# A two-layer decoder step with streamed weights: the stream numbered across layers, fewer semaphore clears, reordered sums, and the rounding of the weights moved from POOL to ACT

## What is computed

```python
mod = (cs @ w_ada[l] + b_ada[l])[:, None, :]
sh_m, sc_m, gt_m, sh_f, sc_f, gt_f = jnp.split(mod, 6, axis=-1)
h = _rmsnorm(x, norm_mix[l]) * (1.0 + sc_m) + sh_m
mix, states = _token_mixers(h, ...)      # h @ w_in, three mixers, gates, @ w_out
x = x + gt_m * mix
h = _rmsnorm(x, norm_ffn[l]) * (1.0 + sc_f) + sh_f
x = x + gt_f * _swiglu(h, w_gate_up[l], w_down[l])
```

## Time and profile before

| | |
|---|---|
| median of three runs | 2710.65 us (2705.59, 2710.65, 2713.01) |
| profiled execution | 2709.27 us, its span 2707.5 |
| mean granted TensorE clock | 0.962 |
| moved by DMA | 263.94 MB, 97 GB/s on average |

### The profile page before, as it was taken

One profiled execution on the slowest core, in us unless ns is written; L12 is line 12 of the kernel. 1 busy time (PEld: TensorE's weight loads), 2 busy tenths in 40 slices (PEclk: granted clock), 3 DMA queues, 4 the chain that ended last, 5 costly groups with the idle time before them and its releaser, 6 DMA issues. The chain is left out here.

```text
span 2707.5 us, 48025 instructions
## 1 busy us (share of the span) xinstructions
PE 2527.8 (93%) x20318; PEld 2412.4 (89%) x20318; DVE 1032.3 (38%) x1481; ACT 456.8 (17%) x856; POOL 1546.9 (57%) x1292
## 2 busy tenths in 40 slices
PE   5989999999999899999969899999999997999997
PEld 3878898989989889999958799889899797999997
DVE  4654414250833442222256634331427435222223
ACT  2432222121021120000024222310211212000000
POOL 2542234557547757777745322356664585777774
PEclk8999998999999999999989899999999998999999
DMA  8730013222423512322256200142141241223222
GB/s 315 242 104 28 28 40 99 81 66 87 113 59 114 223 59 87 86 90 90 79 186 212 73 32 28 47 125 75 63 137 52 57 151 56 90 85 90 88 86 73
DMA packets 167045, 263.94 MB, mean 97 GB/s; under 512 B 14128, under 2 KB 83376, under 8 KB 165040
## 3 DMA queue, kind: packets, MB, share of 16 engines
q1 hardware_dynamic: 166832, 260.88, 30.4%
HBM read 239.65 MB, written 21.17 MB: 96 GB/s over the span
## 5 line engine op out<-in xcount | busy, mean ns | idle before, releaser
L730 PE MATMUL gemm_psum<-h_hi_lo,w_hi_lo 128*128 128x272 f32 x12000 | 1633.1, 295 | 60.2 <-POOL w_hi_lo L707 41.2
L730 PEld LDWEIGHTS gemm_psum<-h_hi_lo,w_hi_lo 128*128 128x128 f32 x12000 | 1561.7, 193 | 107.9 <-issue 52.9
L705 POOL TENSOR_TENSOR w_hi_lo<-w_raw,consts 128x512 fp32r<-128x512 f32 (+1 forms) x644 | 686.2, 1066 | 1080.6 <-PE gemm_psum L730 984.8
L707 POOL TENSOR_TENSOR w_hi_lo<-w_raw,w_hi_lo 128x512 fp32r<-128x512 f32 (+1 forms) x644 | 861.8, 1338 | 50.4
L1894 ACT ACTIVATE tiles<-gemm_psum 128x544 f32<-128x544 f32 (+1 forms) x188 | 116.5, 624 | 1189.6 <-PE gemm_psum L730 1189.0
L730 PE MATMUL gemm_psum<-ffn_hi_lo,w_hi_lo 128*128 128x272 f32 x2112 | 266.5, 288 | 0.0
L730 PEld LDWEIGHTS gemm_psum<-ffn_hi_lo,w_hi_lo 128*128 128x128 f32 x2112 | 266.1, 188 | 0.0
L1876 DVE TENSOR_TENSOR tiles<-gemm_psum,tiles 128x544 f32<-128x544 f32 x44 | 31.9, 725 | 392.9 <-PE gemm_psum L730 392.9
L730 PE MATMUL gemm_psum<-o_hi_lo,w_hi_lo 128*128 128x272 f32 x1152 | 154.0, 290 | 0.0
L730 PEld LDWEIGHTS gemm_psum<-o_hi_lo,w_hi_lo 128*128 128x128 f32 x1152 | 147.1, 189 | 0.0
L1894 ACT ACTIVATE scratch<-mix_psum 128x512 f32<-128x512 f32 (+3 forms) x112 | 58.8, 547 | 367.7 <-PE mix_psum L994 172.8
(11 more groups left out here) (236 smaller groups left out, 1935.9 us busy)
## 6 DMA issues: line engine op xcount, KB each, us to landing
w_raw<-in_w_gu SPq DMA_DIRECT2D x176, 256.0 KB, 2.7
tiles<-in_w_ada SPq DMA_DIRECT2D x64, 512.0 KB, 4.3
w_raw<-in_w_merge SPq DMA_DIRECT2D x96, 256.0 KB, 2.6
w_raw<-in_w_first SPq DMA_DIRECT2D x68, 256.0 KB, 5.1
w_raw<-in_w_ret SPq DMA_DIRECT2D x64, 256.0 KB, 2.7
w_raw<-in_w_hg SPq DMA_DIRECT2D x64, 256.0 KB, 2.7
w_raw<-in_w_dn SPq DMA_DIRECT2D x64, 256.0 KB, 2.6
w_raw<-in_w_merge SPq DMA_DIRECT2D x96, 128.0 KB, 2.1
```

The source lines that it names most:

```text
L705: pool.tensor_tensor(hi, src, ones[:, 0:1].broadcast_to([P, words]), ALU.mult).then_inc(hi_done, 1)
L707: pool.tensor_tensor(lo, src, hi.bitcast(F32), ALU.subtract).then_inc(split_done, 1)
L730: mm = pe.matmul(GP[:, 2 * (tile % 2) + h, 0:HALF], whl[:, n % SLOTS, a, j * P:(j + 1) * P], rhs[:, b, step, h * HALF:(h + 1) * HALF], sta ...
```

## The change

1. *One stream.* Slabs are numbered through both layers. The prologue loads the first four slabs, behind the modulation groups and ahead of `final_norm` and the constants, and POOL splits them there. Layer 0 goes on to load, round and split the first four slabs of layer 1. The parameters are loaded ahead of the groups.
2. *Joins by group.* In the prologue a group's four joins follow its product, into bank 0, which the root must have left. `first_modulation` adds the bias from PSUM to MOD, and `scale_and_gain` makes scale times gain: for layer 0 in the prologue, for layer 1 in layer 0's feed-forward part, for a feed-forward part ahead of its norm. `modulate` begins with L1227's successor.
3. *Clears.* There is none after the prologue and none after layer 1. Between the layers four engines clear 34 semaphores; SP has cleared 57, those of the mixers alone, during the feed-forward part.
4. *Sooner sums.* `add_gated` adds the square of tile i - 1 to the sum ahead of its wait for tile i, where it was behind the addition of tile i.
5. *Rounding on ACT.* ACT's `Feed` starts at tile 0. At each slab's last k-step in its feed it rounds the slab four further on with a Copy to fp32r (`round_slab`), ahead of the evacuation if that step ends a tile. `x_squares` and the feed-forward part get `fill` calls, so that roundings stand there too. POOL only subtracts. The first four slabs are rounded by POOL still.

```diff
+    def join_group(pe, bank, g):
+        for i in range(4 * g, 4 * g + 4):
+            mm = pe.matmul(B[:, bank, i * NJ:(i + 1) * NJ], ADR[:, i * P:(i + 1) * P], join, start=True, stop=True)
+    def first_modulation(dve, k, bank, PR):
+        k.link(dve.tensor_tensor(MOD[:, 0:2 * KD, :], B[:, bank, 0:2 * KD * NJ].rearrange("p (i j) -> p i j", j=NJ),
+                                 PR[:, P_BADA:P_BADA + 2 * KD].unsqueeze(2).broadcast_to([P, 2 * KD, NJ]), ALU.add))
+    def split_slab(pool, n):
...
+        pool.tensor_tensor(hi, src, ones[:, 0:1].broadcast_to([P, words]), ALU.mult).then_inc(hi_done, 1)
+        pool.wait_ge(hi_done, n + 1)
+        pool.tensor_tensor(lo, src, hi.bitcast(F32), ALU.subtract).then_inc(split_done, 1)
...
+            for n in range(SLOTS):
+                load_slab(sp, n)
             sp.dma_start(FN[:, :], fnorm_in[:, :]).then_inc(sig("fnorm_landed"), 16)
...
+        @block.gpsimd
+        def _(pool):
+            pool.wait_ge(sig("ones_landed"), 16)
+            for n in range(SLOTS):
+                split_slab(pool, n)
...
-    def clear():
-        engines = (nc.sync, nc.scalar, nc.vector, nc.gpsimd, nc.tensor)
-        for i, s in enumerate(sems.values()):
+    def clear_layer():
+        engines = (nc.sync, nc.scalar, nc.gpsimd, nc.tensor)
+        for i, s in enumerate(layer_signals):
             engines[i % len(engines)].sem_clear(s)
         nc.all_engine_barrier()
-    clear()
...
+        slab_base = l * len(SLABS)
+        slab_end = min(slab_base + len(SLABS) + SLOTS, DEPTH * len(SLABS))
...
-                for n, (_, _, kt) in enumerate(SLABS):
+                for n in range(slab_base + SLOTS, slab_end):
...
-                    pool.tensor_tensor(hi, src, ones[:, 0:1].broadcast_to([P, words]), ALU.mult).then_inc(hi_done, 1)
                     pool.wait_ge(hi_done, n + 1)
...
                 def add_gated(tile, gate, squares=False):
                     i = TILES[tile][1]
+                    if squares and i >= 2:
+                        sum_square(i - 1)
                     wait_tile(tile)
...
                     if squares:
                         dve.nop().then_inc(sig("x_tile_ready"), 1)
-                        if i >= 2:
-                            sum_square(i - 1)
...
-                feed = Feed(CONV_END)
+                feed = Feed(0)
+                rounded = [slab_base + SLOTS]
+                def round_slab():
+                    n = rounded[0]
+                    if n == slab_end:
+                        return
+                    rounded[0] += 1
+                    words = SLABS[n % len(SLABS)][2] * P
+                    act.wait_ge(slab_done, n - SLOTS + 1)
+                    act.wait_ge(landed[n % SLOTS], landed_by[n])
+                    f(whl[:, n % SLOTS, 0, 0:words], raw[:, n % SLOTS, 0:words], ACT.Copy).then_inc(hi_done, 1)
                 def fill(n, limit):
-                    for tile in feed.whole(n, limit):
-                        evacuate(tile)
+                    for tile, step in feed.take(n, limit):
+                        slab, j, kt = TILES[tile][2][step]
+                        if j == kt - 1:
+                            round_slab()
+                        if tile >= CONV_END and step == len(TILES[tile][2]) - 1:
+                            evacuate(tile)
```

More of the change, by code:

```diff
@@ L435, in trunk @@
     landed_by, total = [], [0] * SLOTS
-    for n, ((name, _), first, _) in enumerate(SLABS):
+    for n in range(DEPTH * len(SLABS)):
+        (name, _), first, _ = SLABS[n % len(SLABS)]
         total[n % SLOTS] += 32 if name.startswith("gate") and first else 16
@@ L691, in _ @@
                         sp.dma_start(ada_group[i], w_ada_first[l + 1, i]).then_inc(sig(f"ada_group_landed_{i}"), 16)
+                if ahead:
+                    drain(BASE["silu1"])
+                    sp.wait_ge(sig("h_ready"), 3 * KD)
+                    for s in mixer_signals:
+                        sp.sem_clear(s)
                 drain(len(TILES))
@@ L1217, in split_samples, with modulate @@
                     return x.rearrange("p i (a t) -> p i a t", a=2)
[L1219 to L1224 removed]
+                def modulate(shift):
                     def scaled(i):
@@ L1354, in modulation @@
                     release(2)
[L1356 to L1359 removed]
+                modulate(0)
                 k.link(dve.tensor_copy(LBC[:, 0, :], LB[:, l, :]))
@@ L2290, in _ @@
                         k.next(sig("ffn_slot_free"))
-                        take(BASE[f"silu{half}"] + 2 * i, FT[:, 0, :], ACT.Silu)
-                x_squares()
+                        tile = BASE[f"silu{half}"] + 2 * i
+                        fill(KD, len(TILES))
+                        take(tile, FT[:, 0, :], ACT.Silu)
+                        fill(KD, len(TILES))
+                    if half == 0:
+                        drain(BASE["silu1"])
+                x_squares(KF, len(TILES))
                 root(RSTD, 1.0 / D, "x_sums")
-        clear()
+        if ahead:
+            clear_layer()
     with nc.Block() as block:
```

105 lines of the change are left out of this document (65 added, 40 removed).

## The result

The changed kernel has a median of 2683.78 us in six runs (2675.41 to 2689.00), beside 2709.06 for the kernel before in six (2700.18 to 2715.00): a ratio of 0.9902, 95% interval 0.9881 to 0.9924. The prediction was 2685. The profiled execution took 2682.55, its span 2680.4, so 27.1 less than the span before.

What follows compares the result with a forecast made beforehand. PE, busy 2527.8 of 2707.5 us, was taken as the bound, so only its roughly 180 us idle could be won. Gains of 28.4 less 4.6 for the roundings gave 24, hence 2685 us, range 2672 to 2701.

Steps and rivals of the forecast that it cites:

- start of the run: Prologue to PE's eighth k-step: 5.6 us from slabs split ahead, 0.7 from an earlier first L1227.
- seam: Between the layers: sooner sums 2.5, fewer clears 1.9, MOD and scale off the path 0.6, slabs split ahead 5.6; together 10.6.
- feed-forward start, layer 1: Layer 1's feed-forward start: earlier root 3.4, scale ahead of the reciprocal 0.3, no POOL splits beside the pattern 1.8.
- feed-forward start, layer 0: Layer 0's feed-forward start: only the scale and the removed POOL splits count, 2.1 us; the sooner sum is hidden.
- end: End of the run: earlier root 0.9, final clears and one of two barriers gone 3.0.
- roundings, net: 640 roundings moved from POOL to ACT: delays in ACT's queue against less slowing of DVE, a loss of 4.6 us.
- the cover of the joins' gain: Prologue: joins by group cut about 3.8 us off DVE's tail, but POOL's splits end later, so costed at nothing.
- its bounds: Roundings' net: 13 places a layer at 0.66 without relief lose 17 us; relief alone gains about 8.
- the prediction's own sign of being wrong: Wrong if mixers' stages, from the eighth step to the first out tile, grow by more than 8 us a layer.
- the rival of DVE's relief: Contended DVE instructions ahead of PE waits end up to 1.0 sooner: 35 us won, 2674; chance 0.12.
- Slabs were ready at every start: Rival: slabs not ready at the starts, twice 5.6 falls away, 12.6 won, 2697; chance 0.06.
- ACT's queue as the chain of the whole run: Rival: evacuations behind roundings come 0.66 late on PE's path, 23 us slower, 2732; chance 0.04.

Runs made afterwards that it cites:

- second profile: The change itself, unedited, run and profiled a second time: median 2677.12 us in five runs, ratio 0.9898 to the kernel before.
- seven profiles with the change's order: Profiles of kernels in which ACT rounds the mixers' slabs ahead of the evacuation, as in the change: mixers 1642.0 to 1651.6 us over both layers, mean 1646.8.
- the joins at once: The change with the prologue's sixteen joins in one piece again behind the last group: 2683.44 us in a single execution.

## Why the prediction was right, by its steps

| term | predicted | measured (first profile) |
|---|---|---|
| first L1227 at | 42.0 | 42.06 |
| start of the run | 6.3 | 6.3 |
| seam | 10.6 | 10.6 |
| feed-forward start, layer 1 | 5.5 | 5.6 |
| feed-forward start, layer 0 | 2.1 | 2.1 |
| end | 3.9 | 4.1 |
| sum of the gains | 28.4 | 28.7 |
| roundings, net | -4.6 | -1.7 |

**The gains** came as costed, since each had its rows: the pattern of 13.6, the 0.12 of a clear, and POOL in the prologue, which took 9.4 (31.75 to 41.14) where 9.7 were costed. POOL was the cover of the joins' gain, and taking it away won 2.0. The gain at layer 1's feed-forward start hangs in part on POOL's shorter work, as the prediction had it: with POOL rounding everything 2.3 of it went. The sooner sums were read as order alone, 2.5 in the seam and 0.9 at the end, and that these came out was luck in part: the kernel before happened to have its ones-matmuls at the lower clock in the seam and at the upper at the end, and with the old order in the changed kernel it was the reverse (1.0 and 2.5).

**The net of the roundings** was the weak step. The two halves were named, their places and sizes were not right. The mixers lost 8.3 in the first profile and 0.9 in the second. Outside them the out projections came out 2.7 and 1.4 shorter and the feed-forward parts 1.1 and 1.5 (-8.3 + 6.6 = -1.7). Of these, POOL's second instruction, put back, took the out projections' 2.5 and 1.3 away again, but none and 0.7 of the feed-forward parts'; what shortened those otherwise is not shown. The prediction took a rounding's price as 0.3 to 0.66 at a place, and expected PE's waits after rope tiles to grow by 0.3 to 0.7. The first rope tile with the change:

```profile
180.84 0.72 DVE L1350 TENSOR_TENSOR tiles<-gemm_psum,consts 128x544 f32<-128x544 f32 x1 [2.22 <-ACT tiles L1948]
...
181.49 0.72 DVE L1352 TENSOR_TENSOR tiles<-tiles,consts 128x544 f32<-128x544 f32 x1
...
185.74 3.33 PE L816 MATMUL mix_psum<-consts,tiles 128*128 128x128 f32 x16 [2.81 <-DVEq L1258]
```

DVE does wait 0.5 longer for ACT (2.22, before 1.72), but PE behind it waits 0.6 less (2.81, before 3.42). It waits 2.81 here in both layers of all seven profiles with the change's order, and 3.26 in both layers of the three changed kernels in which POOL rounds the mixers' slabs, so at this place DVE's relief wins 0.45. Two prices were missing: a table load that can't pass the rounding (1.28 more), and the clock behind a longer wait, which made one 1.85 into 6.6 in some profiles. That the net lay within its bounds was thus no merit of its sizes: with the second profile's mixers it is +5.7. And the prediction's own sign of being wrong, mixers longer by more than 8 us in a layer, was missed by little in the first profile (7.6), while a later kernel with the same mixers crossed it (11.3, the joins at once).

**The rivals.** With 2683.78 and, the second time, 2677.12 the result lies between the forecast and the rival of DVE's relief (2674). Slabs were ready at every start; ACT's queue as the chain of the whole run can be ruled out: ACT still waits for PE 1269.8 us ahead of its roundings. The rule of the Trainium skill ("SBUF — State Buffer", section "SBUF: two separate sides") that the prediction set beside its rows held: L1352's 1.85 beside a subtraction of 1.28, and DVE's 122 us less where POOL only subtracts (1015.8 to 894.0).

**What stays open**: what the move costs the mixers as a whole. Its mean of 3.7 rests on four and seven profiles.

## What to carry to other kernels

Price a moved instruction by what it stops from running early (a table load, an evacuation) and by where the work that follows it lands, not by its own length. Read a gain in a stage where one chain ends all waits from rows, and it comes out to a tenth or two, as long as the engine's clock is the same in both; in a stage where an engine waits often and its granted clock falls behind some of the waits, profile the same program twice before a difference of a few microseconds is put down to an edit. After a change of several parts, look for the wait that it left: here one that it did not touch was worth as much as a third of it.

## What was not expected

One program gave mixers of 833.0 and 822.6 us in two profiles, with every stretch outside them equal to 0.3: the difference is k-steps of 1.71 or 0.99 us, twelve matmuls of 3.07 or 1.75, at either level of the granted clock. The two profiles were 0.2 us apart when these mixers began. The same order of instructions with the same wait of 1.6 in front was followed by k-steps at the lower clock at seven of fourteen places and not at the others; what tips the clock was not isolated.
